# A hybrid encoder trunk on one core: gate projections as one stacked pass, attention inputs fetched block by block

## The chip, the cores and the metric

The kernel runs on one core of a Trainium2 chip. The metric is the device time of one execution, in microseconds. The engines named below are TensorE (PE in the rows; PEld is its weight load), VectorE (DVE), ScalarE (ACT), GpSimd (POOL) and SyncE (SP), which only issues transfers. ScalarE issues transfers too, in the same queue as its computing.

## What is computed

Two groups of tokens (512 and 256, together 768 in six tiles of 128) go through two layers and a final RMSNorm, all in fp32. A layer:

```python
h = rmsnorm(x, norm_g)
proj = h @ w_in
qa, ka, va, gfl, gbl, za, qb, kb, vb, zb, ma, mb = split(proj)
gf = log_sigmoid(gfl @ w_gate_f + b_gate_f) / 16     # rank 16 -> 512, forward decay
gb = log_sigmoid(gbl @ w_gate_b + b_gate_b) / 16     # the same for the backward direction
# branch A: gated linear attention, 4 heads (key 128, value 256), both directions
ya = (rmsnorm(o_forward + o_backward) * silu(za)) @ w_branch_a
# branch B: grouped-query attention, 16 query and 4 key heads of 64, RMSNorm and rotary on q, k
yb = (attention(rope(rmsnorm(qb)), rope(rmsnorm(kb)), vb) * silu(zb)) @ w_branch_b
x = x + (sigmoid(ma) * ya + sigmoid(mb) * yb) @ w_out
```

The gate path matters here: `gfl` and `gbl` have 16 columns each (32 together), and a small product takes them to 128 decays per head and direction. The other path is the one that prepares branch B: `q` and `kv` are read back from DRAM, squared, and summed over each head of 64.

## The kernel before

**Products in two parts.** A large product takes each operand as a high part (rounded to fp32r) and a low part (the rest), and makes three fp32r passes: high x high, high x low, low x high (`three_passes`, L510 to L512). Weights come through a ring of four slots. SyncE loads `w_raw`, ScalarE writes `w_hi` (`split`, L794), GpSimd writes `w_lo` (L1151), TensorE uses them and signals `w_used`. Weights are three blocks ahead (`SKEW = 3`). Smaller products are plain fp32, which shows as two records for each matmul.

**The gate projection.** A layer begins with `gemm_features(1)`: 128 columns of `w_in`, of which 32 are gate columns, in banks 6 and 7. VectorE copies 32 rows of the result to `gl_t` (L1536). Then follow the projections for `q`, `k` (`gemm_features(4)`) and `v` of branch A.

**The gate product.** `gla_gates` multiplies `gl_t` (32 rows) by the small weights `wg_fix` of one head in plain fp32:

```python
for d, start, n in ((0, 0, HALF), (0, HALF, TOK - HALF), (1, 0, TOK - HALF), (1, TOK - HALF, HALF)):
    z = 2 * HALF + d * TOK + start
    last = mm(ps[:, z:z + n], wg_fix[:, d, :], gl_t[:, start:start + n], start=True, stop=True)   # L594
```

GpSimd cuts `wg_fix` and the bias `bg_fix` out for each head (`gla_fix`). The first head's product stands alone in the gate stage, where ScalarE turns it into decays (`gate_magnitudes` L852, exponential, logarithm, exponential), with splits of background weights in between. Those of heads 1 to 3 run in level 3 of the head before.

**A linear-attention head** has ten levels (`GLA_STEPS`, n = 0 to 9). In level n TensorE makes a score product (L621, L609 in the last), then background tiles: the projections of branch B, `GLA_DONE` says up to which tile (4 in level 0, 11 in levels 1 to 5, then 10 or 11, 6 in the last). VectorE collects the product (`collect`, L1358 to L1365) and scales queries and keys for the next level (`doubled`, L1344 to L1350); ScalarE merges the keys (`merge_k`, L882), on which the next level's product waits. After level 9 VectorE drains and signals `a_ready` (L1388), and `gla_values` (L636) makes the head's output. Splits of background weights are spread over the levels (`GLA_START`), and in level 5 ScalarE stores a finished group of the background (`store`, L799 three times, then a DMA to `proj` in DRAM) before `merge_k`.

**The last head** also prepares branch B. In level 2 ScalarE issues everything at once in `fetch_qk`: four loads of `q`, two of `kv` (L816, 768 KB each), and four small parameters (L820) for the rope tables. From level 4 on it squares one token tile per level (`squares_of`, three ACTIVATEs, L904) and VectorE sums it (`square_sums`, L1435). The rope tables are made in level 3. The last tile's sums stand ahead of the drain for `a_ready`.

ScalarE, VectorE and GpSimd each work through their instructions in the order in which they are written; nothing overtakes a waiting one.

## Time and profile before

| | |
|---|---|
| median of 3 runs | 2178.04 us (2176.38 to 2178.86) |
| the profiled execution | 2178.59 us, span 2176.80 |
| TensorE busy | 2058.8 us, 95% of the span |
| ScalarE, VectorE, GpSimd busy | 858.1, 835.1, 659.3 us |
| mean granted clock of TensorE | 0.974 of full |
| moved by DMA | 157.07 MB, mean 72 GB/s |

Busy shares are means over stages with different limits, so they are read by stretch. The granted clock is given as a share of 2.4 GHz. A matmul's duration in a timeline overlaps its successor's; the pace is read from the distance between starts, or from the chain that ended last.

### The profile page before, as it was taken

To read this page: it belongs to the slowest core of one execution; us is meant where nothing else is said; L and a number is where in the kernel's file an instruction comes from. 1 tells how busy PE (TensorE), PEld (TensorE's weight loads), DVE (VectorE), ACT (ScalarE), POOL (GpSimd) and SP (SyncE) were. 2 spreads that over 40 slices of the span, in tenths; PEclk is the share of its full clock that TensorE was granted. 3 is DMA by queue.
4 is the path that set the end of the run, shared out by engine and by line. 5 is a ranking of instruction groups with operands and counts; after the bars stand their busy time and mean duration, and the time that the engine had idled before them with its cause. 6 is when DMAs were issued, how large, how long until landed. Compare 5 with 4: busy or idle time off the path is not lost.

```text
span 2176.8 us, 39353 instructions
## 1 busy us (share of the span) xinstructions
PE 2058.8 (95%) x13792; PEld 1896.9 (87%) x13792; DVE 835.1 (38%) x1158; ACT 858.1 (39%) x1712; POOL 659.3 (30%) x697
## 2 busy tenths in 40 slices
PE   5999999899999999999879999998999999999996
PEld 4988999899999998877779889998999999988785
DVE  3012555469432332323131035455693333323323
ACT  4113454443445454423221145444334555544222
POOL 1322222138432231322223322221583321213221
PEclk8999999999999999999979999999999999999998
DMA  3221212422111113331122111124221111142312
GB/s 122 68 58 49 66 53 63 149 70 65 53 43 41 58 43 127 117 117 54 34 69 61 51 54 61 60 68 142 76 61 45 44 58 39 60 145 87 113 59 84
DMA packets 116300, 157.07 MB, mean 72 GB/s; under 512 B 12960, under 2 KB 88992, under 8 KB 116192
## 3 DMA queue, kind: packets, MB, share of 16 engines
q1 hardware_dynamic: 78480, 96.18, 15.5%
q10 hardware_dynamic: 37712, 59.52, 7.8%
q8 instruction: 60, 0.98, 0.2%
q14 instruction: 48, 0.39, 0.1%
HBM read 124.20 MB, written 31.46 MB: 72 GB/s over the span
## 4 chain that ended last, share of the span: by engine, by line
PE 78%; issue 8%; POOL 6%; DVE 4%; ACT 2%; ACTq 1%; DMA 1%; DVEq 1%; POOLq 0%; SPq 0%
PE ps L510 10%; PE ps L512 10%; PE ps L511 10%; PE ps L548 8%; PE ps L550 8%; PE ps L549 8%; PE ps L691 6%; PE ps L621 5%; PE ps L636 3%; POOL w_lo L1151 3%; PE ps L675 3%; POOL rot L1190 2%; PE ps L574 2%; PE ps L667 2%; PE ps L668 2%
## 5 line engine op out<-in xcount | busy, mean ns | idle before, releaser
L1151 POOL TENSOR_TENSOR w_lo<-w_raw,w_hi 128x256 fp32r<-128x256 f32 (+2 forms) x531 | 525.2, 997 | 1466.9 <-ACT w_hi L794 1452.9
L548 PE MATMUL ps<-w_hi,act_hi 128*128 128x256 f32 x2112 | 625.5, 296 | 9.8 <-POOL w_lo L1151 7.0
L549 PE MATMUL ps<-w_lo,act_hi 128*128 128x256 f32 x2112 | 600.0, 284 | 0.0
L550 PE MATMUL ps<-w_hi,act_lo 128*128 128x256 f32 x2112 | 599.9, 284 | 0.0
L794 ACT ACTIVATE w_hi<-w_raw 128x256 fp32r<-128x256 f32 (+2 forms) x528 | 251.2, 485 | 583.8 <-PE ps L512 363.6
L548 PEld LDWEIGHTS ps<-w_hi,act_hi 128*128 128x128 f32 x2112 | 407.3, 193 | 15.1 <-POOL w_lo L1151 7.6
L549 PEld LDWEIGHTS ps<-w_lo,act_hi 128*128 128x128 f32 x2112 | 407.6, 193 | 0.6
L550 PEld LDWEIGHTS ps<-w_hi,act_lo 128*128 128x128 f32 x2112 | 406.7, 193 | 0.0
L1489 DVE TENSOR_REDUCE st<-ps 128x1 f32<-128x512 f32 (+1 forms) x160 | 110.4, 690 | 249.2 <-PE ps L668 248.2
L961 ACT ACTIVATE pr_t<-ps 128x512 f32<-128x512 f32 x160 | 95.6, 597 | 217.5 <-PE ps L675 217.5
L691 PE MATMUL ps<-v_grp,pr_t 128*128 128x64 f32 x1280 | 161.8, 269 | 1.4 <-DVE q L1495 1.4
L510 PE MATMUL ps<-w_hi,o_hi 128*128 128x512 f32 x384 | 154.8, 403 | 6.2 <-DVE o_lo L1297 3.3
L691 PEld LDWEIGHTS ps<-v_grp,pr_t 128*128 128x128 f32 x1280 | 156.8, 192 | 2.8 <-issue 2.8
L512 PE MATMUL ps<-w_hi,o_lo 128*128 128x512 f32 x384 | 150.6, 392 | 0.0
L511 PE MATMUL ps<-w_lo,o_hi 128*128 128x512 f32 x384 | 150.3, 391 | 0.0
L882 ACT ACTIVATE scaled<-scaled 128x768 f32<-128x768 f32 x64 | 53.3, 833 | 206.3 <-DVE scaled L1344 180.1
L953 ACT ACTIVATE pr<-ps,st 128x512 f32<-128x512 f32 (+1 forms) x192 | 116.9, 612 | 31.2 <-DVE st L1489 31.2
L621 PE MATMUL ps<-scaled 128*128 128x128 f32 x768 | 108.2, 294 | 16.7 <-ACT scaled L882 16.7
L621 PEld LDWEIGHTS ps<-scaled 128*128 128x128 f32 x768 | 100.9, 200 | 21.9 <-ACT scaled L882 17.3
L1360 DVE COPY_PREDICATED amat<-mask,ps 128x768 f32<-128x768 uint8 x56 | 58.0, 1036 | 134.7 <-PE ps L621 99.1
L510 PE MATMUL ps<-act_hi,w_hi 128*128 128x384 f32 x288 | 99.1, 344 | 6.3 <-DVEq L442 3.5
L511 PE MATMUL ps<-act_lo,w_hi 128*128 128x384 f32 x288 | 98.3, 341 | 0.0
(151 smaller groups left out, 3230.6 us busy)
## 6 DMA issues: line engine op xcount, KB each, us to landing
w_raw<-in_w_in SPq DMA_DIRECT2D x352, 128.0 KB, 2.1
proj<-stg ACTq DMA_DIRECT2D x36, 768.0 KB, 3.3
w_raw<-in_w_in SPq DMA_DIRECT2D x64, 256.0 KB, 2.7
w_raw<-in_w_branch_a SPq DMA_DIRECT2D x32, 256.0 KB, 2.6
w_raw<-in_w_branch_b SPq DMA_DIRECT2D x32, 256.0 KB, 2.6
w_raw<-in_w_out SPq DMA_DIRECT2D x32, 256.0 KB, 2.5
q<-proj ACTq DMA_DIRECT2D x8, 768.0 KB, 8.1
zb<-proj ACTq DMA_DIRECT2D x8, 768.0 KB, 7.3
```

Of the source, the lines that this page charges most:

```text
L510: mm(out, s_hi, m_hi, start=first, stop=False)
L511: mm(out, s_hi, m_lo, start=False, stop=False)
L512: return mm(out, s_lo, m_hi, start=False, stop=last)
L548: mm(out, act_hi[:, k, tok], w_hi[:, k % RING, 0:BGW], start=(k == 0 and t % 2 == 0), stop=False, skip_group_check=True)
L549: mm(out, act_hi[:, k, tok], w_lo[:, k % RING, 0:BGW], start=False, stop=False, skip_group_check=True)
L550: last = mm(out, act_lo[:, k, tok], w_hi[:, k % RING, 0:BGW], start=False, stop=(k == KT - 1), skip_group_check=True)
L621: last = mm(ps[:, j * P:(j + 1) * P], lhs, rhs, start=True, stop=True)
L691: last = mm(ps[:, 3 * HALF + t * DH:3 * HALF + (t + 1) * DH], pr_t[:, n % 2, (i * 2 + j) * P:(i * 2 + j + 1) * P], v_grp[:, key, :], start ...
L794: A(w_hi[:, slot, 0:width], w_raw[:, slot, 0:width], ACT.Copy).then_inc(s.w_hi_done, 1)
L953: last = A(pr[:, n % 2, i * w:(i + 1) * w], ps[:, n % 2 * HALF + i * w:n % 2 * HALF + (i + 1) * w], ACT.Exp, bias=nmax(n, i), accum_out=de ...
L1151: G.tensor_tensor(w_lo[:, slot, 0:width], w_raw[:, slot, 0:width], w_hi[:, slot, 0:width].bitcast(F32), ALU.subtract).then_inc(s.w_lo_done, 1)
L1489: V.tensor_reduce(out, view_ps(n % 2 * HALF, (HALF // k, k), (1, HALF // k)), AX.X, ALU.max, negate=True).then_inc(s.neg_max, 1)
```

## The change

Three things.

1. The gate projection loads 32 columns instead of 128 and stacks them: the 128 stationary columns hold the high part three times and the low part once (`gate_split`). One pass with the high part of the input and one with its low part replace the three passes (`gemm_gates`). The result has 128 rows.
2. `gl_t` and `wg_fix` become 128 rows of fp32r: rows 32 to 63 of `gl_t` hold what rounding took away, rows 64 to 95 of `wg_fix` the low part of the weights. The gate product is then one fp32r pass. The weights are loaded four times over (eight parameters instead of two), VectorE and GpSimd each get a chained subtraction.
3. In the last head the parameters are loaded in level 0, and the six blocks of `q` and `kv` one per level from level 1 to 6; each level waits for the block of the level before, and squares it as one column block over all six tiles. VectorE sums one block per level in levels 3 to 7, the rope tables move to level 8, and nothing is left ahead of `a_ready`.

```diff
-    gl_t = sb("gl_t", [2 * RANK, TOK], R_O + 11 * ROW)
+    gl_t = sb("gl_t", [P, TOK], R_O + 11 * ROW, F32R)
...
-    wg_fix = sb("wg_fix", [2 * RANK, 2, GK], R_G + NT * BGW * 4)
-    wg = sb("wg", [2 * RANK, 2, GH * GK], R_G + NT * BGW * 4 + 2 * GK * 4)
+    wg_fix = sb("wg_fix", [P, 2, GK], R_G + NT * BGW * 4, F32R)
+    wg = sb("wg", [P, 2, GH * GK], R_G + NT * BGW * 4 + 2 * GK * 4)
...
-                load_group(w_in, layer, C_GATES, P)
+                load_group(w_in, layer, C_GATES, GR)
...
-            def gemm_features(blocks):
+            def gemm_gates():
 
                 for k in range(KT):
                     pe.wait_ge(s.w_lo_done, at("w_lo_done"))
-                    for b in range(8 - 2 * blocks, 8):
+                    for half in range(2):
+                        if k == 0:
+                            pe.wait_ge(s.drained, at.peek("drained", half - 1))
+                        tok = slice(half * FH, (half + 1) * FH)
+                        mm(bank(6 + half, FH), w_hi[:, k % RING, 0:P], act_hi[:, k, tok], start=(k == 0), stop=False)
+                        last = mm(bank(6 + half, FH), w_hi[:, k % RING, 0:P], act_lo[:, k, tok], start=False, stop=(k == KT - 1))
+                        if k == KT - 1:
+                            last.then_inc(s.gemm_ready, 1)
+                    (last if k < KT - 1 else pe.drain()).then_inc(s.w_used, 1)
+                at.skip("drained", 2)
+
+            def gemm_features():
+
+                for k in range(KT):
...
-                gemm_features(1)
+                gemm_gates()
                 with at.repeat(2, "gla qk"):
-                    gemm_features(4)
+                    gemm_features()
...
+            def gate_split(k):
+
+                slot = (k + SKEW) % RING
+                act.wait_ge(s.w_slot[slot], at(f"w_slot{slot}", 16))
+                act.wait_ge(s.w_used, at("w_used"))
+                A(view(w_hi, slot * HALF, (GR, 3), (1, GR)), view(w_raw, slot * HALF, (0, 3), (1, GR)), ACT.Copy).then_inc(s.w_hi_done, 1)
...
-            def fetch_qk():
-
-                act.wait_ge(s.totals, at.peek("totals", 1))
-                all_stored()
-                for c in range(4):
-                    fetch(q, J_Q + c, c * BGW, D, 1, s.qkv_in)
-                for c in range(2):
-                    fetch(kv, J_K + c, c * BGW, HALF, 1, s.qkv_in)
-                param(cs_raw[:, 0, :, :], rope_cos)
-                param(cs_raw[:, 1, :, :], rope_sin)
-                param(g_qk[:, 0, :], rows_of(q_norm_g, layer * DH, DH))
-                param(g_qk[:, 1, :], rows_of(k_norm_g, layer * DH, DH))
-
-            def squares_of(t):
-
-                if t == 0:
-                    act.wait_ge(s.qkv_in, at("qkv_in", 6 * 16))
-                for part in range(3):
-                    src = view(q, t * D + part * HALF, (1, HALF)) if part < 2 else view(kv, t * HALF, (1, KVH * DH))
+            def fetch_qk(n):
+
+                if n == 0:
+                    param(cs_raw[:, 0, :, :], rope_cos)
+                    param(cs_raw[:, 1, :, :], rope_sin)
+                    param(g_qk[:, 0, :], rows_of(q_norm_g, layer * DH, DH))
+                    param(g_qk[:, 1, :], rows_of(k_norm_g, layer * DH, DH))
+                if n == 1:
+                    act.wait_ge(s.totals, at.peek("totals", 1))
+                    all_stored()
+                if n >= 2:
+                    act.wait_ge(s.qkv_in, at("qkv_in", 16))
+                if 1 <= n < 5:
+                    fetch(q, J_Q + n - 1, (n - 1) * BGW, D, 1, s.qkv_in)
+                if 5 <= n < 7:
+                    fetch(kv, J_K + n - 5, (n - 5) * BGW, HALF, 1, s.qkv_in)
+                if 2 <= n < 7:
+                    c = n - 2
+                    src = view(q, c * BGW, (D, NT), (1, BGW)) if c < 4 else view(kv, 0, (HALF, NT), (1, BGW))
                     act.wait_ge(s.sq_used, at("sq_used"))
-                    A(bank(2 + part, HALF if part < 2 else KVH * DH), src, ACT.Square).then_inc(s.sq_ready, 1)
+                    A(view_ps(2 * HALF, (BGW, NT), (1, BGW)), src, ACT.Square).then_inc(s.sq_ready, 1)
...
-                    if not more and n == 2:
-                        fetch_qk()
...
-                    if not more and 4 <= n:
-                        squares_of(n - 4)
+                    if not more and n < 8:
+                        fetch_qk(n)
...
-                param(wg[0:RANK, 0, :], bass.AP(w_gate_f.tensor, layer * (RANK * GH * GK), [[GH * GK, RANK], [1, GH * GK]]))
-                param(wg[RANK:2 * RANK, 1, :], bass.AP(w_gate_b.tensor, layer * (RANK * GH * GK), [[GH * GK, RANK], [1, GH * GK]]))
+                    if k + SKEW < KT:
+                        gate_split(k)
+                    else:
+                        split(k)
...
+            def gate_split(k):
+
+                slot = (k + SKEW) % RING
+                pool.wait_ge(s.w_hi_done, at("w_hi_done"))
+                G.tensor_tensor(w_hi[:, slot, 3 * GR:4 * GR], w_raw[:, slot, 0:GR], w_hi[:, slot, 0:GR].bitcast(F32),
+                                ALU.subtract).then_inc(s.w_lo_done, 1)
...
-                G.tensor_copy(wg_fix[:], view_32(wg, h * GK, (GH * GK, 2), (1, GK)))
                 G.tensor_copy(bg_fix[:], view(bg, h, (GH, 2)))
+                G.tensor_copy(wg_fix[:], view(wg, h * GK, (GH * GK, 2), (1, GK))).then_inc(s.pool_chain, 1)
+                pool.wait_ge(s.pool_chain, at("pool_chain"))
+                pool.sem_inc(s.passed, 1)
+                rows = slice(2 * GR, 3 * GR)
+                G.tensor_tensor(wg_fix[rows], view_rows(wg, 2 * GR, GR, h * GK, (GH * GK, 2), (1, GK)),
+                                wg_fix[rows].bitcast(F32), ALU.subtract)
                 pool.drain().then_inc(s.gla_fix, 1)
...
-                    if not more and n == 3:
+                    if not more and 3 <= n < 8:
+                        square_sums(n - 3)
+                    if not more and n == 8:
                         dve.wait_ge(s.param, at("param", 4 * 16))
                         dve.sem_inc(s.passed, 1)
                         rope_tables()
-                    if not more and 5 <= n:
-                        square_sums(n - 5)
-                if not more:
-                    square_sums(NT - 1)
                 at.skip("q_ready", 1)
...
-            def square_sums(t):
-
-                for part in range(3):
-                    heads = 8 if part < 2 else KVH
-                    stat = t * AH + part * 8 if part < 2 else NT * AH + t * KVH
-                    dve.wait_ge(s.sq_ready, at("sq_ready"))
-                    V.tensor_reduce(view(st_qk, stat, (1, heads)), view_ps((2 + part) * HALF, (DH, heads), (1, DH)),
-                                    AX.X, ALU.add).then_inc(s.sq_used, 1)
+            def square_sums(c):
+
+                dve.wait_ge(s.sq_ready, at("sq_ready"))
+                out = view(st_qk, c * GROUP, (AH, NT), (1, GROUP)) if c < KVH else view(st_qk, NT * AH, (KVH, NT), (1, KVH))
+                V.tensor_reduce(out, view_ps(2 * HALF, (BGW, NT), (DH, GROUP), (1, DH)), AX.X, ALU.add).then_inc(s.sq_used, 1)
...
-                    V.tensor_copy(gl_t[:, half * FH:(half + 1) * FH], ps[0:2 * RANK, (6 + half) * HALF:(6 + half) * HALF + FH]).then_inc(s.drained, 1)
+                    tok = slice(half * FH, (half + 1) * FH)
+                    V.tensor_copy(gl_t[:, tok], bank(6 + half, FH)).then_inc(s.dve_chain, 1)
+                    dve.wait_ge(s.dve_chain, at("dve_chain"))
+                    V.tensor_tensor(gl_t[GR:2 * GR, tok], ps[GR:2 * GR, (6 + half) * HALF:(6 + half) * HALF + FH],
+                                    gl_t[GR:2 * GR, tok].bitcast(F32), ALU.subtract).then_inc(s.drained, 1)
...
+                for copy in range(4):
+                    for d, w_gate in enumerate((w_gate_f, w_gate_b)):
+                        row = copy * GR + d * RANK
+                        param(wg[row:row + RANK, d, :], bass.AP(w_gate.tensor, layer * (RANK * GH * GK), [[GH * GK, RANK], [1, GH * GK]]))
```

## Rows read from the trace of the kernel before

**Rows 1.** Windows: busy time of each engine, granted clock, DMA share, GB/s.
```profile
270.00:330.00 60.00, 59.97 (x449) 57.13 (x449) 31.49 (x38) 29.61 (x52) 14.52 (x18) 1.00 0.19 58
390.00:450.00 60.00, 51.09 (x395) 50.00 (x394) 32.79 (x51) 22.90 (x52) 10.53 (x15) 0.94 0.45 141
```

**Rows 2.** Waits of TensorE over the whole span: us in total, times, longest.
```profile
PE ps L621 <- ACT scaled L882: 16.7, 3, 8.3
...
PE ps L636 <- DVEq L1388: 4.7, 2, 2.4
```

**Rows 3.** Timeline, ScalarE's queue in the last head, level 2.
```profile
403.03 3.25 ACTq L816 DMA_DIRECT2D q<-proj  x4
406.31 5.44 ACTq L816 DMA_DIRECT2D kv<-proj  x2
...
415.85 0.84 ACT L882 ACTIVATE scaled<-scaled 128x768 f32<-128x768 f32 x1 [13.05 <-issue]
```

**Rows 4.** Timeline, TensorE: head 1 to the start of head 2, then the last head.
```profile
272.41 1.50 PE L621 MATMUL ps<-qk_t,scaled 128*128 x12
...
286.52 1.50 PE L621 MATMUL ps<-scaled 128*128 128x128 f32 x12
...
291.90 2.84 PE L594 MATMUL ps<-gl_t,wg_fix 32*128 32x512 f32 x8
294.67 1.60 PE L621 MATMUL ps<-scaled 128*128 128x128 f32 x12
...
333.32 1.50 PE L621 MATMUL ps<-qk_t,scaled 128*128 x12
...
394.24 1.50 PE L621 MATMUL ps<-qk_t,scaled 128*128 128x128 f32 x12
...
467.88 0.38 PE L548 MATMUL ps<-w_hi,act_hi 128*128 128x256 f32 x1 [0.37 <-issue]
```

**Rows 5.** Chain that ended last, products of 384 columns: start, us.
```profile
48.30 0.17 PE ps L510
```

**Rows 6.** The same chain, products of 512 columns.
```profile
116.83 0.23 PE ps L511
```

**Rows 7.** Timeline of the gate stage, ScalarE and TensorE.
```profile
187.06 1.69 ACT L852 ACTIVATE gate<-ps,bg_fix 128x768 f32<-128x768 f32 x2 [7.41 <-PE ps L594]
...
202.33 0.58 PE L548 MATMUL ps<-w_hi,act_hi 128*128 128x256 f32 x1 [2.90 <-POOL w_lo L1151]
```

**Rows 8.** DMA issues: KB each, median us from issue to landing.
```profile
q<-proj ACTq DMA_DIRECT2D x8, 768.0 KB, 8.1
...
ma<-proj ACTq DMA_DIRECT2D x8, 768.0 KB, 4.7
...
kv<-proj ACTq DMA_DIRECT2D x4, 768.0 KB, 11.2
...
w_raw<-in_w_in SPq DMA_DIRECT2D x19, 64.0 KB, 1.9
```

**Rows 9.** Windows behind the gate product in head 0 of layer 2.
```profile
1308.00:1310.00 2.00, 2.00 (x11) 2.00 (x11) 0.16 (x1) 0.00 (x0) 0.00 (x0) 0.50 0.00 0
1310.00:1312.00 2.00, 2.00 (x16) 2.00 (x16) 2.00 (x3) 0.28 (x1) 0.00 (x0) 0.82 0.00 0
```

**Rows 10.** Timeline, ScalarE and VectorE in levels of head 1 and the last head.
```profile
298.33 0.85 ACT L882 ACTIVATE scaled<-scaled 128x768 f32<-128x768 f32 x1 [6.26 <-DVE scaled L1344]
...
422.73 0.34 DVE L1420 TENSOR_TENSOR cs<-cs_raw,g_qk 128x192 f32<-128x192 f32 x1
...
426.38 1.04 DVE L1360 COPY_PREDICATED amat<-mask,ps 128x768 f32<-128x768 uint8 x1 [0.34 <-DVEq L1426]
...
430.68 1.55 ACT L799 ACTIVATE stg<-ps 128x512 f32<-128x512 f32 x3
...
433.75 1.61 DVE L1435 TENSOR_REDUCE st_qk<-ps 128x8 f32<-128x512 f32 x3
...
434.46 1.20 ACT L904 ACTIVATE ps<-q 128x512 f32<-128x512 f32 x2
```

More of the change, by code:

```diff
@@ L53 @@
 RANK = 16
+GR = 2 * RANK
 GATE_NORM = 16.0
@@ L353, in view, with view_rows @@
         return bass.AP(t, start, [[row, P]] + [list(d) for d in dims])
+    def view_rows(t, first, n, start, *dims):
+        row = 1
+        for size in t.shape[1:]:
+            row *= size
+        return bass.AP(t, first * row + start, [[row, n]] + [list(d) for d in dims])
     def rows_of(a, start, n):
@@ L495, in _ @@
                         load_group(w, layer, g * HALF)
-            load_group(w_in, 0, C_GATES, P, blocks=SKEW)
+            load_group(w_in, 0, C_GATES, GR, blocks=SKEW)
             for t in range(NT):
@@ L552, in background @@
                         last.then_inc(s.w_used, 1)
-            def gemm_features(blocks):
+            def gemm_gates():
                 for k in range(KT):
                     pe.wait_ge(s.w_lo_done, at("w_lo_done"))
-                    for b in range(8 - 2 * blocks, 8):
+                    for half in range(2):
[10 more added lines that the diff above has]
+                for k in range(KT):
+                    pe.wait_ge(s.w_lo_done, at("w_lo_done"))
+                    for b in range(8):
                         if k == 0:
                             pe.wait_ge(s.drained, at.peek("drained", b + 1 - 8))
-                        col = slice((b // 2 + blocks - 4) * P, (b // 2 + blocks - 3) * P)
+                        col = slice(b // 2 * P, (b // 2 + 1) * P)
                         tok = slice(b % 2 * FH, (b % 2 + 1) * FH)
@@ L567, in gemm_features @@
                     (last if k < KT - 1 else pe.drain()).then_inc(s.w_used, 1)
-                at.skip("drained", 2 * blocks)
+                at.skip("drained", 8)
             def turn_step(src, m):
@@ L1126, in _ @@
                 for k in range(KT):
-                    split(k, HALF if k + SKEW < KT else P)
+                    if k + SKEW < KT:
+                        split(k)
+                    else:
+                        gate_split(k)
                     if k == 1:
@@ L1226, in _ @@
             for k in range(SKEW):
-                split(k - SKEW, P)
+                gate_split(k - SKEW)
             with at.repeat(DEPTH, "layer"):
@@ L1232, in _ @@
                 for k in range(KT):
-                    split(k, P if k + SKEW < KT else HALF)
+                    if k + SKEW < KT:
+                        gate_split(k)
+                    else:
+                        split(k)
                 with at.repeat(4, "gla projections"):
                     splits()
-                pool.wait_ge(s.param, at("param", (2 + 2 * GH) * 16))
+                pool.wait_ge(s.param, at("param", (8 + 2 * GH) * 16))
                 pool.sem_inc(s.passed, 1)
@@ L1259, in _ @@
                 for k in range(KT):
-                    split(k, HALF if k + SKEW < KT else P)
+                    if k + SKEW < KT:
+                        split(k)
+                    else:
+                        gate_split(k)
                 phase_ends()
```

30 lines of the change are left out of this document (12 added, 18 removed).

## The prediction

> **What bounds the kernel now.** I read the busy shares by stretch first. In an ordinary linear-attention head TensorE is busy 59.97 of 60 us; in the stretch of the last head of the layer it is busy only 51.09 of 60, while the DMA share goes from 0.19 to 0.45 [rows 1]. So in ordinary heads, time goes only if TensorE work goes; in the last head something else sets the end.
>
> The waits say what. TensorE stands at L621 (the score product of a level) for the ScalarE copy L882 (`merge_k`), 8.3 us at the longest, once in each of the two layers, and at L636 (`gla_values`) for VectorE's queue, 2.4 us, once in each [rows 2]. The timeline of ScalarE's queue shows the cause of the first. From 403.03 on it issues four loads of `q` (3.25 us) and two of `kv` (5.44 us), then the four parameters of the rope tables until 415.85, where the next L882 runs [rows 3]. L882 stood behind 12.8 us of issuing, in a queue full of its own transfers, while VectorE had long scaled its input. The second wait is the block of `square_sums` that VectorE still has ahead of the drain that feeds `a_ready`.
>
> How much is that in all? I compare whole heads by the starts of TensorE work [rows 4]. Head 1 runs from 272.41 to the next head's first product at 333.32, 60.91 us, of which the gate product L594 takes 294.67 - 291.90 = 2.77 us; the last head has none. So an undisturbed last head should take 58.14 us. It takes 467.88 - 394.24 = 73.64 us, of which 0.37 is the drain behind it. Excess: 73.64 - 0.37 - 58.14 = 15.1 us. The two waits give 10.7 of it; the rest is the lower clock after each of them and a small stall at the store. The second layer repeats both waits with the same lengths [rows 2].
>
> **Part 1, the gate projection.** Before: 8 blocks x 2 halves x 3 passes = 48 matmuls of 384 columns. After: two passes, 32. At full clock one takes 0.17 us of the chain [rows 5]; the stretch at half clock with which the group starts I take to be equally long with either count, so the 16 that go are priced at full clock: 16 x 0.17 = 2.7 us, **5.4 us** in two layers. (If they went at half clock it would be twice that, which the range holds.) Is something late instead? The three-deep ring of split weights: the copy and the subtraction get narrower, and the first wide block is ordered several blocks ahead; I find it ready about when the gates end, inside the half microsecond that TensorE spends on its drain and loop between the groups. The loads become 32 columns (128 B a row) instead of 128. One of 64 KB lands after 1.9 us now [rows 8], and the last narrow one has over 4 us before its split is due; at twice 1.9 us it would still be in time. If the first wide block is late by all of one copy and subtraction, 1 us a layer is lost: the bounds of this part are 3.4 and 5.4, and I take the upper.
>
> VectorE's two drains become four short instructions; they free banks 6 and 7, which the next group needs only after 18 matmuls (18 x 0.17 = 3.1 us). Without that cover the two added ones would cost about 1 us. ScalarE issues eight weight parameters instead of two. Even in the full queue of rows 3 four parameters took 4.1 us (411.75 to 415.85), so six more cost at most 6.2 us; what is queued behind them is the split of the next group's fourth block, which TensorE wants after three blocks of 24 matmuls, 72 x 0.17 = 12 us. GpSimd's `gla_fix` gains a chained wait and a subtraction, an estimated 1 to 2 us; it runs in level 1 and L594 comes at the end of level 3, two levels later. All of these at nothing.
>
> **Part 2, the gate product L594.** It is now a plain fp32 product over 32 rows, 1,536 columns, 2.77 us [rows 4]. After, it is one fp32r product over 128 rows with the same columns. An fp32r product of 512 columns takes 0.23 us of the chain [rows 6], so 1,536 take 0.69 us. Saved: 2.08 us each. Six lie in heads where TensorE is full: **12.5 us**. Two lie in the gate stage, where the chain begins with them: ScalarE's L852 waits for L594 at 187.06, and TensorE later waits 2.90 us for a split that stands behind that chain, until 202.33 [rows 7]. The chain starts 2.08 us earlier and keeps its length: **4.2 us**. The bounds are 0 (if the new form ran at the old rate) and 2.77 us each (if it vanished); I take 2.08 because every other fp32r product of the trace runs at this pace.
>
> **Part 3, the clock.** Outside stretches with idle time, the granted clock falls three times in the trace, each time at or right behind an L594 (near 187, 1307 and 1431 us; one of the three stands in the rows). With TensorE busy 2.00 of 2.00 it shows 0.50, the lower of its two levels (1.2 of 2.4 GHz), then 0.82 on the way back [rows 9]: (0.50 + 0.18) x 2 = 1.4 us lost. Two of these lie in full heads. The new product fills all rows and is four times shorter, so I expect no fall: **2.8 us**, between 0 and 3.2.
> The Trainium skill, "TensorE: Matmul & The Clock Gate", section "Seeing it yourself", shows the clock falling after matmuls have stopped, and its section "What's actually happening" ties it to how busy TensorE has been. Read as idle time alone, this term would be 0 and the time 2129; the rows, which fall without idle time, disagree with that reading.
>
> **Part 4, the last head.** Six transfers of 768 KB are now issued one at a time, one per level from level 1 on; ScalarE waits for the last one before it issues the next; the four parameters come in level 0. Does each transfer fit into a level? A level takes 291.90 - 286.52 = 5.4 us of TensorE, 1.5 of it the score product [rows 4]. Six at once land after 8.1 us (`q`) and 11.2 us (`kv`); `ma`, fetched with spacing and in the same form, after 4.7 us [rows 8]. ScalarE comes back to the wait one level later, about 5.0 us after the issue. So it nearly never waits. Its queue then holds, per level, L882 0.85, up to two splits (an estimated 0.8), an issue (0.5) and one square of 1,536 columns: two of 512 take 1.20 us now [rows 10], so three times 512 in one, about 1.5 us. L882 is wanted 298.33 - 294.67 = 3.7 us after its level's score product begins [rows 4, 10]; ScalarE, held until then by the second split and the square, is free at about 2.1 to 2.5 us. One place doesn't fit: level 5 begins with the store (three copies, 1.55 us [rows 10]), which stands behind the square of level 4, which stands behind VectorE's sum of the block before. VectorE's sum ends about 1.65 + 3.0 + 1.6 = 6.2 us into level 4, the square 1.5 us later, 2.3 us after the next level's score product has started; the first bank is copied at about 2.9, and TensorE wants it at 1.5. New stall: 1.4 us, against 0.5 now (estimates, all of them).
>
> VectorE: five sums of 1,536 columns at about 1.6 us (three reduces of a tile take 1.61 us [rows 10]) instead of six; with an estimated 3.3 us of level work that is 4.9 us, under 5.4. The rope tables take 3.65 us with their drain, from 422.73 to the copy at 426.38 [rows 10]; they move to level 8, where VectorE has about as much time free before it must take up the last product; an estimated 0.4 us late at most, and `a_ready` then comes just as TensorE arrives, since the reduces ahead of it are gone. So of 15.1 us, 1.4 stay: 13.7 x 2 = **27.4 us**. Bounds: nothing saved (the transfers land as late as now) to 30.2.
>
> **Sum.** 5.4 + 12.5 + 4.2 + 2.8 + 27.4 = 52.3 us. The profiled execution took 2178.59 (span 2176.80 and 1.79 around it): 2126.3. It was 0.55 above the median of 2178.04: 2125.7. I say 2126.
>
> **The rivals.**
> *The fetches set the pace of the last head.* ScalarE's loop is then: a transfer lands, the next is issued, square, copy, wait. A level can't be shorter than one landing. With 8.1 us, the present median of `q`, six levels are 2.8 us longer, less about 3 of slack: 14 us a layer, which takes back the 27.4: about 2153. For it: ScalarE waits in order and weights are loaded beside it. Against: the long landings are those of six in flight at once. In a mild form (5.9 us) it costs 1 to 2 us a layer and is in my range. 0.12.
> *The same, and slower than before.* At a landing of 11.2 us, `kv`'s median, six levels are 5.9 us longer each, 32 us a layer after slack: 64 - 52.3 = 12 us slower, 2190. It decides from about 10.2 us of landing on. That number exists only with six in flight. 0.02.
> *The heads don't give the time back.* If VectorE and ScalarE really pace the levels, the 12.5 and 2.8 us go: 2141. Against: 59.97 of 60, and no L621 waits in those heads [rows 1, 2]. 0.08.
> *The clock stays as it is.* Falls go on after the gate product (2.8 us), and the new stall in level 5 brings one of about 2 us in each layer: 2133. 0.18.
> *As forecast.* 0.60, by itself 2121 to 2131.
>
> The range takes in the clock rival and the mild fetch rival and stops short of the strong one: 2118 to 2144. What a measurement of this kernel can tell from no change is 0.2%, 4.4 us; of the cases only the fetch rival at a landing near 10.2 us comes there, and I leave it 0.01. Faster 0.97, same 0.01, slower 0.02.
>
> **What would show it.** L594 as four records of about 0.7 us together per head; heads of about 58.8 us from first product to first product, equal in both layers; no wait at L621 for L882 over 1 us; ScalarE's issues of `q` and `kv` at 0.4 to 0.6 us each, landing under 5.5; no wait at L636; a stall of about 1.4 us at the first background matmul after the level-5 product; granted clock 1.00 throughout the last head. Wrong would make it: landings of 7 us or more, a level-5 stall that lowers the clock, or a gate stage whose chain starts no earlier because the wider `gla_fix` ends it.

## The result, and the profile after

The changed kernel takes 2124.3 us (median of 4 runs, 2122.36 to 2125.05) against 2178.45 us for the kernel before on the same chip: a ratio of 0.9752, with a 95% interval of 0.9735 to 0.9769. That is 54 us saved where 52 were forecast. The profiled execution took 2124.74 us, its span is 2122.9 us against 2176.8, and its mean granted clock 0.983 against 0.974.

I cut both traces at the same instructions (first gate matmul, first q/k/v matmul, gate product, first score product of each head, first matmul behind the last head) and subtracted. Two numbers in a cell are the two layers; three are heads 0, 1 and 2.

| stretch | before, us | after, us | saved in all | forecast |
|---|---|---|---|---|
| gate projection | 11.35, 11.98 | 9.20, 7.93 | 6.2 | 5.4 |
| q, k, v projections | 136.65, 136.56 | 136.68, 136.65 | -0.1 | 0 |
| gate stage (gate product to first score product) | 27.33, 26.17 | 24.38, 24.16 | 5.0 | 4.2 |
| heads 0 to 2 of layer 1 | 60.93, 60.91, 60.92 | 58.73, 58.65, 58.64 | 6.7 | 12.5 + 2.8 = 15.3 for both layers |
| heads 0 to 2 of layer 2 | 62.22, 60.92, 62.23 | 58.72, 58.67, 58.66 | 9.3 | (in the row above) |
| last head with the drain behind it | 73.64, 73.55 | 59.92, 59.92 | 27.35 | 27.4 |
| all the rest | | | -0.5 | 0 |

The busy time in windows of 60 us (engine busy time with the number of instructions, then the granted clock, the DMA share and GB/s) is read as in [rows 1], for the changed kernel, first around an ordinary head and then in the last one:

```profile
270.00:330.00 60.00, 59.97 (x461) 58.44 (x461) 32.74 (x40) 29.63 (x52) 16.63 (x21) 1.00 0.20 61
380.00:440.00 60.00, 58.52 (x449) 57.01 (x448) 39.55 (x53) 28.07 (x51) 11.97 (x16) 1.00 0.47 149
```

TensorE was busy 51.09 us in such a stretch of the last head and is busy 58.52 now; the 1.48 us that is missing is one stall, in the next fence. The ordinary head was full and is full: it got shorter by the 2.06 us of work that left it, and by 0.2 us beside that work.

TensorE's timeline (start, busy time, line, operation, tiles, count, and in brackets the idle time ahead of it with its releaser), answers to [rows 4]: the gate product is one group of four, and from its start to that of its successor it takes 284.47 - 283.76 = 0.71 us where it was 2.77. The last head begins at 381.64 and the first matmul behind it is at 441.56.

```profile
283.76 0.87 PE L616 MATMUL ps<-gl_t,wg_fix 128*128 128x512 f32 x4
284.47 1.50 PE L643 MATMUL ps<-scaled 128*128 128x128 f32 x12
...
381.64 1.50 PE L643 MATMUL ps<-qk_t,scaled 128*128 128x128 f32 x12
...
406.35 1.50 PE L643 MATMUL ps<-scaled 128*128 128x128 f32 x12
...
409.33 0.38 PE L555 MATMUL ps<-w_hi,act_hi 128*128 128x256 f32 x1 [1.48 <-ACT stg L828]
...
441.56 0.38 PE L555 MATMUL ps<-w_hi,act_hi 128*128 128x256 f32 x1 [0.34 <-issue]
```

No score product (L643) waits for `merge_k` (L911) any more, and no `gla_values` matmul (L658) for VectorE's queue; [rows 2] had 16.7 and 4.7 us there. Of TensorE's waits in these stages these entries of the list of waits remain (us in total, times, longest): the splits of the gate stage, and the stores, of which the two of 1.48 us, one in each last head, are the longest.

```profile
PE ps L555 <- POOL w_lo L1184: 8.6, 4, 3.6
...
PE ps L555 <- ACT stg L828: 4.5, 4, 1.5
```

ScalarE's queue in levels 1 to 5 of the last head answers to [rows 3]. An issue takes 0.38 to 0.41 us instead of 8.7 us for six in a row, `merge_k` waits for its data and not for issuing, and one square of 1,536 columns takes 1.46 us:

```profile
390.45 0.41 ACTq L845 DMA_DIRECT2D q<-proj  x1
394.02 0.85 ACT L911 ACTIVATE scaled<-scaled 128x768 f32<-128x768 f32 x1 [3.63 <-DVE scaled L1392]
...
395.33 0.40 ACTq L845 DMA_DIRECT2D q<-proj  x1
395.77 1.46 ACT L933 ACTIVATE ps<-q 128x1536 f32<-128x1536 f32 x1
...
405.88 0.38 ACTq L845 DMA_DIRECT2D q<-proj  x1
407.31 1.45 ACT L933 ACTIVATE ps<-q 128x1536 f32<-128x1536 f32 x1 [1.55 <-DVE st_qk L1479]
408.70 1.55 ACT L828 ACTIVATE stg<-ps 128x512 f32<-128x512 f32 x3
```

The square that starts at 407.31 had waited 1.55 us for VectorE's sum; the store's copies (L828) stand behind it, and TensorE stands behind the first of them. The DMA issues (size of one, median time from issue to landing) answer to [rows 8]: 8.1 and 11.2 us became 4.8 and 4.9.

```profile
q<-proj ACTq DMA_DIRECT2D x8, 768.0 KB, 4.8
...
kv<-proj ACTq DMA_DIRECT2D x4, 768.0 KB, 4.9
...
w_raw<-in_w_in SPq DMA_DIRECT2D x19, 16.0 KB, 1.8
```

### The profile page after: what moved, and what is told of

Its sections match the earlier page's. It is cut to its first block, busy times and chain, and to the rows that moved or that the text cites. A ratio compares the mean times of both kernels' runs of the same rounds, so it can differ in the third digit from the quotient of the medians.

```text
span 2122.9 us, 39205 instructions
## 1 busy us (share of the span) xinstructions
PE 2023.0 (95%) x13728; PEld 1872.6 (88%) x13728; DVE 836.0 (39%) x1136; ACT 854.8 (40%) x1686; POOL 662.2 (31%) x705
## 3 DMA queue, kind: packets, MB, share of 16 engines
q10 hardware_dynamic: 38096, 59.92, 8.2%
## 4 chain that ended last, share of the span: by engine, by line
PE 81%; issue 6%; POOL 6%; DVE 3%; ACT 2%; DMA 1%; DVEq 0%; ACTq 0%; SPq 0%; POOLq 0%
PE ps L517 10%; PE ps L519 10%; PE ps L518 10%; PE ps L555 8%; PE ps L557 8%; PE ps L556 8%; PE ps L713 6%; PE ps L643 5%; PE ps L658 3%; PE ps L697 3%; POOL w_lo L1184 3%; POOL rot L1232 2%; PE ps L596 2%; PE ps L689 2%; PE ps L690 2%
## 5 line engine op out<-in xcount | busy, mean ns | idle before, releaser
L1184 POOL TENSOR_TENSOR w_lo<-w_raw,w_hi 128x256 fp32r<-128x256 f32 (+1 forms) x512 | 515.7, 1016 | 1324.0 <-ACT w_hi L816 1322.1
L816 ACT ACTIVATE w_hi<-w_raw 128x256 fp32r<-128x256 f32 (+1 forms) x512 | 246.1, 490 | 545.5 <-PE ps L519 321.8
L911 ACT ACTIVATE scaled<-scaled 128x768 f32<-128x768 f32 x64 | 53.3, 833 | 162.4 <-DVE scaled L1392 161.3
L643 PE MATMUL ps<-scaled 128*128 128x128 f32 x768 | 102.4, 283 | 0.0
L643 PEld LDWEIGHTS ps<-scaled 128*128 128x128 f32 x768 | 96.8, 192 | 0.3
L697 PE MATMUL ps<-ident,pr 128*128 128x128 f32 x640 | 95.9, 272 | 0.0
L517 PEld LDWEIGHTS ps<-w_hi,o_hi 128*128 128x128 f32 x384 | 72.9, 190 | 24.2 <-issue 5.8
```

The lines of the kernel that those rows point to most:

```text
L517: mm(out, s_hi, m_hi, start=first, stop=False)
L643: last = mm(ps[:, j * P:(j + 1) * P], lhs, rhs, start=True, stop=True)
L697: last = nc.tensor.transpose(ps[:, 2 * HALF + j * P:2 * HALF + (j + 1) * P], pr[:, n % 2, j * P:(j + 1) * P], ident[:])
L816: A(w_hi[:, slot, 0:width], w_raw[:, slot, 0:width], ACT.Copy).then_inc(s.w_hi_done, 1)
L1184: G.tensor_tensor(w_lo[:, slot, 0:width], w_raw[:, slot, 0:width], w_hi[:, slot, 0:width].bitcast(F32), ALU.subtract).then_inc(s.w_lo_done, 1)
```

## The experiments

Beside these runs the kernel before took 2176.0 to 2177.1 us, beside the changed kernel 2178.45. Where a run is compared with the changed kernel's 2124.3 below, the difference in time is therefore good to about 2 us; the stretches of the traces are finer. The diffs are cut to the lines that carry the change, and `...` marks a cut.

**One half of the change each.** The first kernel has the new gate path and the old fetch; the second the old gate path and the new fetch. The diff is the first one's edit on ScalarE; on VectorE `square_sums` and `rope_tables` go back to their old levels. The second is the kernel before with the reverse of it.

```diff
+                    if not more and n == 2:
+                        fetch_qk()
...
-                    if not more and n < 8:
-                        fetch_qk(n)
+                    if not more and 4 <= n:
+                        squares_of(n - 4)
```

> The stacked gate projection and the fp32r gate product, with the fetches and squares of the last head as they were. If the parts simply add, by the step lengths of the two traces: gate projection 6, gate stage 5, heads 16, so 27 us faster than before (about 2151), and the last head keeps its wait of 8.3 us at the level-3 product and its 2.4 us ahead of the values. Rival (the parts cover one another: a shorter chain gives the last head more or less to wait for): the last head's 73.6 us change by more than 1 us.

> The fetches and squares block by block, with the gate projection in three passes and the gate product in plain fp32 over 32 rows. If the parts add: 27 us faster than before (about 2151), last head 59.9 us. The plain gate product is there again eight times: my theory of the clock says that one to four of them are followed by a granted clock of 0.50 while TensorE is busy. The rival (the falls came by chance or from the idle times elsewhere) says none in a second profile.

The gate path alone: 2149.71 us against 2177.08, ratio 0.9874 (0.9851 to 0.9897), 27.4 us less. The fetch alone: 2150.27, ratio 0.9875 (0.9859 to 0.9892), 26.8 us less. Together 54.2 us, what the whole change gives: as times the halves add up. In the first kernel both waits of [rows 2] are still there, from its list of waits:

```profile
PE ps L643 <- ACT scaled L911: 15.8, 3, 7.9
...
PE ps L658 <- DVEq L1438: 4.7, 2, 2.4
```

Its last heads take 73.08 and 71.57 us, 0.56 and 1.98 less than before, so 2.5 us of the last head's gain are to be had by the gate path too: the wait is 0.4 us shorter, and in layer 2 the clock does not fall a second time behind the wait for `a_ready`. In the second kernel the other heads take 60.93 to 60.94 us, and one 62.24, as before, and its last heads 59.95 and 59.92: the fetch alone gives the whole of that term. As stretches the halves add less neatly than as times. The 2.5 us are in both; against them, the stretch from the last head of layer 1 to the gate projection of layer 2, whose code is the same everywhere, takes 644.9 and 645.6 us in the two kernels against 642.1 before and 644.4 after.

**The gate product: type or rows?** The 128 stacked rows stay, the operands are plain fp32. (The subtractions then give zeros in the rows for the low parts; the product's value is that of plain fp32.)

```diff
-    gl_t = sb("gl_t", [P, TOK], R_O + 11 * ROW, F32R)
+    gl_t = sb("gl_t", [P, TOK], R_O + 11 * ROW)
...
-    wg_fix = sb("wg_fix", [P, 2, GK], R_G + NT * BGW * 4, F32R)
+    wg_fix = sb("wg_fix", [P, 2, GK], R_G + NT * BGW * 4)
```

> The changed kernel with the gate product in plain fp32 over 128 rows (64 of them hold zeros, since nothing is rounded away; the result is the same sum). It separates length from rows. Price of the plain product: 8 x 2.06 = 16.5 us slower than the changed kernel (about 2141). On the clock: if the 32 used rows made it fall, it stays at 1.00 behind all eight products; if the 2.8 us of plain fp32 made it fall, it falls behind some of them and heads with a fall are about 1.4 us longer.

2137.38 us, ratio 0.982 (0.9803 to 0.9836): 13.1 us slower than the changed kernel, where 16.5 were expected. Between the starts of its neighbours the product now takes 2.58 us, from TensorE's timeline:

```profile
285.70 2.74 PE L616 MATMUL ps<-gl_t,wg_fix 128*128 128x512 f32 x8
288.28 1.50 PE L643 MATMUL ps<-scaled 128*128 128x128 f32 x12
```

Its heads take 60.53 us, 1.88 more than 58.65, and the gate stages 26.27 and 26.25, 1.9 and 2.1 more: 15.2 us; its gate projections are 1.4 us shorter, because their first matmuls run at half clock for less time. So of the 2.06 us per product the type gives 1.87, and 0.19 comes from filling the rows: the plain product over 32 rows is slower than the plain product over 128. No run shows why.

**Three passes again in the gate projection.**

```diff
                         mm(bank(6 + half, FH), w_hi[:, k % RING, 0:P], act_hi[:, k, tok], start=(k == 0), stop=False)
+                        mm(bank(6 + half, FH), w_hi[:, k % RING, 0:P], act_lo[:, k, tok], start=False, stop=False)
                         last = mm(bank(6 + half, FH), w_hi[:, k % RING, 0:P], act_lo[:, k, tok], start=False, stop=(k == KT - 1))
```

(It adds the low part of the input once too often.)

> The changed kernel with a third pass in the stacked gate projection (the product with the low part of the input is added twice, so the output is not the reference's). It prices the 16 matmuls alone. At full clock: 2.7 us a layer, 5.4 in all, gate projection 2.7 us longer in both layers. Rival: the lengths of the two layers (9.2 and 7.9 us now) move by different amounts, because the time at half clock at the start of the group varies by more than the matmuls cost.

2129.38 us, ratio 0.9782 (0.9765 to 0.9798), 5.1 us slower. The projections take 10.78 and 10.90 us against 9.20 and 7.93: 1.6 and 3.0 us more, unequal, as the rival said, and 4.6 in all. Of the eighteen projections of nine kernels with the short form, fourteen take 7.7 to 8.6 us, three 9.1 to 9.2 and one 6.6; their mean is 8.1, that of the six of three kernels with three passes 11.05. The difference is how much of one runs at half clock, as the windows of the changed kernel at the start of the group show (the granted clock is the third number from the end), layer 1 and then layer 2:

```profile
36.00:38.00 2.00, 2.00 (x8) 2.00 (x7) 0.00 (x0) 0.28 (x1) 0.25 (x1) 0.50 0.06 12
38.00:40.00 2.00, 2.00 (x7) 2.00 (x7) 0.00 (x0) 0.57 (x2) 0.29 (x2) 0.50 0.45 126
40.00:42.00 2.00, 2.00 (x9) 2.00 (x9) 0.00 (x0) 0.34 (x2) 0.46 (x2) 0.62 0.76 166
...
1086.00:1088.00 2.00, 2.00 (x6) 2.00 (x7) 0.00 (x0) 0.48 (x2) 0.25 (x1) 0.50 0.06 11
1088.00:1090.00 2.00, 2.00 (x9) 2.00 (x9) 0.00 (x0) 0.35 (x2) 0.51 (x2) 0.65 0.24 34
```

The share of the last row gives the moment of the return: layer 1 stays at half clock until about 41.5, 6.2 us into the group (0.62 is 1.5 us at 0.50 and 0.5 at 1.00), layer 2 until about 1089.4, 3.4 us into it.

**Six transfers at once, but in the new places.** All six are issued in level 1. Squares and sums follow one level later than in the changed kernel, and the rope tables stand in level 3 instead of 8 (VectorE's part of the edit is not shown).

```diff
-                if n >= 2:
-                    act.wait_ge(s.qkv_in, at("qkv_in", 16))
-                if 1 <= n < 5:
-                    fetch(q, J_Q + n - 1, (n - 1) * BGW, D, 1, s.qkv_in)
-                if 5 <= n < 7:
-                    fetch(kv, J_K + n - 5, (n - 5) * BGW, HALF, 1, s.qkv_in)
-                if 2 <= n < 7:
-                    c = n - 2
+                    for c in range(4):
+                        fetch(q, J_Q + c, c * BGW, D, 1, s.qkv_in)
+                    for c in range(2):
+                        fetch(kv, J_K + c, c * BGW, HALF, 1, s.qkv_in)
+                if n == 3:
+                    act.wait_ge(s.qkv_in, at("qkv_in", 6 * 16))
+                if 3 <= n < 8:
+                    c = n - 3
```

> The changed kernel with all six fetches issued together in level 1, one wait for all of them in level 3, squares in levels 3 to 7, rope tables in level 3. Nothing waits for a landing before level 3. If the issuing itself stalls ScalarE (its queue is full of its own transfers, 8.7 us for six in the trace of before), the level-2 key copy comes 4 to 6 us late, TensorE waits 3 to 5 us for it in each layer, and the kernel is 6 to 10 us slower than the changed one. If the old stall came from waiting for the landings, this form costs nothing: same as the changed kernel.

2138.56 us, ratio 0.9829 (0.9814 to 0.9844), 14 us slower than the changed kernel. ScalarE's queue shows the block of issuing back, and `merge_k` behind it (8.97 us in which ScalarE's computing waited for nothing that the profile shows but its own issues):

```profile
389.41 3.35 ACTq L845 DMA_DIRECT2D q<-proj  x4
392.79 5.42 ACTq L845 DMA_DIRECT2D kv<-proj  x2
398.32 0.84 ACT L911 ACTIVATE scaled<-scaled 128x768 f32<-128x768 f32 x1 [8.97 <-issue]
```

```profile
399.22 2.07 PE L643 MATMUL ps<-scaled 128*128 128x128 f32 x8 [4.33 <-ACT scaled L911]
...
415.52 0.39 PE L555 MATMUL ps<-w_hi,act_hi 128*128 128x256 f32 x1 [2.17 <-ACT stg L828]
```

The second fence is TensorE's timeline of the same kernel: 4.33 us of waiting, and 2.17 us at the store. The last heads take 68.61 and 66.86 us, 8.7 and 6.9 more. The direction is that of the theory, and the wait of 4.33 us is in its range of 3 to 5. The size, 6 to 10 us, was forecast too small: the lower clock behind the wait and the price of the tables' new place were not in it. The next kernel has squares, sums and tables in the same levels as this one and differs only in how they are issued and waited for; it is 10.7 us faster, timed in the same comparison, and that is about the price of six at once against pairs.

**Two at a time.** Pairs are issued in levels 1, 3 and 5; squares, sums and tables stand where they did in the run above.

```diff
+                if n in (3, 5, 7):
+                    act.wait_ge(s.qkv_in, at("qkv_in", 2 * 16))
+                if n in (1, 3):
+                    for c in (n - 1, n):
+                        fetch(q, J_Q + c, c * BGW, D, 1, s.qkv_in)
+                if n == 5:
+                    for c in range(2):
+                        fetch(kv, J_K + c, c * BGW, HALF, 1, s.qkv_in)
```

> The changed kernel with the fetches issued in pairs in levels 1, 3 and 5, waited for two levels later, squares in levels 3 to 7, rope tables in level 3. If only a full queue makes issuing slow, a pair costs 0.8 to 1 us, there is no wait for the key copy, and the time is that of the changed kernel within 2 us. If each issue beside another transfer stalls (2 us or more), 1 to 3 us slower per layer.

2127.84 us, ratio 0.9775 (0.976 to 0.979), 3.5 us slower. From its ScalarE timeline, a pair is issued in 1.00 us, and it lands after 5.8 us (`q`) and 6.4 us (`kv`):

```profile
390.41 1.00 ACTq L845 DMA_DIRECT2D q<-proj  x2
```

No wait of TensorE stands behind a pair. Yet the last heads take 62.75 and 61.19 us, 2.8 and 1.3 more: the level-5 product waits 0.40 us for `merge_k`, and the store stall is 2.17 us instead of 1.48. Neither comes from the fetches. VectorE makes the rope tables in level 3 here, and what follows in its queue is late: the next collecting copy starts at 403.99, where it is 402.69 in the changed kernel. ScalarE's `merge_k` waits for VectorE behind that, and so does the square ahead of the store; in layer 1 the clock then falls behind the stall besides. VectorE's row first, then ScalarE's:

```profile
403.99 1.03 DVE L1410 COPY_PREDICATED amat<-mask,ps 128x768 f32<-128x768 uint8 x1 [0.35 <-DVEq L1474]
405.89 0.84 ACT L911 ACTIVATE scaled<-scaled 128x768 f32<-128x768 f32 x1 [2.46 <-DVE scaled L1394]
```

**The splits of the gate stage.** This goes beyond the change. In the changed kernel TensorE stands 0.77 and 3.54 us in each gate stage for the subtraction that follows a split:

```profile
191.59 0.38 PE L555 MATMUL ps<-w_hi,act_hi 128*128 128x256 f32 x1 [0.77 <-POOL w_lo L1184]
...
197.54 0.39 PE L555 MATMUL ps<-w_hi,act_hi 128*128 128x256 f32 x1 [3.54 <-POOL w_lo L1184]
```

```diff
                 split(0, BGW)
                 gate_exps()
-                gate_logs()
                 split(1, BGW)
+                gate_logs()
+                split(2, BGW)
                 copy_k(0)
+                split(3, BGW)
                 gate_decays()
-                for i in range(2, GLA_FIRST // NT):
+                for i in range(4, GLA_FIRST // NT):
```

> The changed kernel with the gate stage of ScalarE in another order: split 1 ahead of the logarithm, split 2 behind it, split 3 ahead of the last exponential. In the changed kernel TensorE waits 0.77 and 3.54 us there for splits queued behind table loads, and runs about 3 us at half clock behind it. I expect both waits gone and the decay chain 0.5 to 1 us later: 4 to 6 us a layer, 8 to 12 us in all (about 2114). Rival: the decay chain sets the end of the stage, the wait moves to the level-1 product, and nothing is gained.

2114.75 us, ratio 0.9715 (0.9701 to 0.9728), 9.6 us below the changed kernel. The gate stages take 19.18 and 19.17 us, 5.1 less on average; a wait of 0.87 us is left in each. The waits give 3.4 us of it; the rest is the clock, which stays at 1.00 in both stages now and was at 0.50 for 3.4 us behind the longer wait in the changed kernel. The splits had stood in ScalarE's order behind the logarithms and the decays, for which they have no need.

**No square in level 4.** On top of that order, level 4 has no square, so that nothing stands ahead of the store in level 5; the tables move to level 5.

```diff
-                if 2 <= n < 7:
-                    c = n - 2
+                if n in (2, 3, 5, 6, 7):
+                    c = n - 2 if n < 4 else n - 3
...
-                    if not more and 3 <= n < 8:
-                        square_sums(n - 3)
-                    if not more and n == 8:
+                    if not more and n in (3, 4, 6, 7, 8):
+                        square_sums(n - 3 if n < 5 else n - 4)
+                    if not more and n == 5:
```

> As the run with splits earlier, and no square in level 4 of the last head: squares in levels 2, 3, 5, 6, 7, sums in 3, 4, 6, 7, 8, rope tables in level 5. The stall of 1.48 us at the store goes (3 us in both layers). VectorE is about 1.5 us over its level in level 5; with slack behind it I expect at most 0.5 us of wait. 2 to 3 us faster than with splits earlier, too little for the times to tell, but the waits in the profile show it. Rival: the tables in level 5 bring a wait for the key copy as long as the stall that goes.

2112.7 us, ratio 0.9705 (0.9692 to 0.9719). The last heads take 58.97 and 58.96 us, 0.95 less. The store stall of 1.48 us is gone and a smaller one took its place, at the level-6 product. It is the wait that the rival named, at over a third of the size: `merge_k` waits for VectorE, which stood at the rope tables in level 5. VectorE, ScalarE and TensorE in turn:

```profile
409.55 1.03 DVE L1410 COPY_PREDICATED amat<-mask,ps 128x768 f32<-128x768 uint8 x1 [0.35 <-DVEq L1474]
411.45 0.84 ACT L911 ACTIVATE scaled<-scaled 128x768 f32<-128x768 f32 x1 [3.63 <-DVE scaled L1394]
412.43 1.58 PE L643 MATMUL ps<-scaled 128*128 128x128 f32 x12 [0.56 <-ACT scaled L911]
```

This is the fastest of all: 64 us below the kernel before, 11.6 below the changed one and 2 below the run with the splits earlier (a distance that single runs of the two overlap; the stretches carry it).

**The clock: length or rows?** The product after is both shorter and wider, so its clock proves nothing on which of the two did it. Both kernels here are that with plain fp32 and do the four matmuls three times over, which gives the same values; the second uses only rows 0 to 31, which leaves the low part of the weights out. The second pair of lines is the second kernel's alone:

```diff
-                for d, start, n in ((0, 0, HALF), (0, HALF, TOK - HALF), (1, 0, TOK - HALF), (1, TOK - HALF, HALF)):
+                for _ in range(3):
+                    for d, start, n in ((0, 0, HALF), (0, HALF, TOK - HALF), (1, 0, TOK - HALF), (1, TOK - HALF, HALF)):
...
-                        last = mm(ps[:, z:z + n], wg_fix[:, d, :], gl_t[:, start:start + n], start=True, stop=True)
+                        last = mm(ps[:, z:z + n], wg_fix[0:GR, d, :], gl_t[0:GR, start:start + n], start=True, stop=True)
```

> The run with plain fp32 over 128 rows, with the gate product made three times in each place (same operands, same output). So far the clock fell behind 6 of 16 plain products over 32 rows and behind 0 of 8 over 128 rows, each 2.8 us long. If the used rows decide, the clock stays at 1.00 behind all eight, though TensorE now does plain fp32 for 8.3 us at a time. If the length of plain fp32 decides, it falls behind most of the eight.

> The same, with only the first 32 rows of both operands in the product (the part of the gate input that came through the low half of the weights is left out). Everything else is as in its partner. If the used rows decide, the clock falls behind all eight or all but one, with TensorE busy throughout, and each head is over 1.5 us longer than its partner's. If it is chance, both runs look alike.

128 rows: 2182.11 us, ratio 1.0026 (1.0015 to 1.0038). 32 rows: 2222.35 us (2 runs), ratio 1.0217 (1.0169 to 1.0264), 40 us more. Windows of 2 us of one head, first the kernel with 128 rows (the next product starts at 238.55), then that with 32 (all four within the product):

```profile
236.00:238.00 2.00, 2.00 (x8) 1.30 (x7) 0.00 (x0) 0.00 (x0) 0.00 (x0) 1.00 0.00 0
238.00:240.00 2.00, 2.00 (x15) 1.64 (x14) 0.00 (x0) 0.00 (x0) 0.00 (x0) 1.00 0.00 0
```

```profile
238.00:240.00 2.00, 2.00 (x8) 1.29 (x7) 0.00 (x0) 0.00 (x0) 0.04 (x1) 1.00 0.48 131
240.00:242.00 2.00, 2.00 (x5) 1.11 (x4) 0.00 (x0) 0.00 (x0) 0.00 (x0) 0.55 0.00 0
242.00:244.00 2.00, 2.00 (x5) 1.19 (x4) 0.00 (x0) 0.00 (x0) 0.00 (x0) 0.50 0.00 0
244.00:246.00 2.00, 2.00 (x3) 0.66 (x2) 0.00 (x0) 0.00 (x0) 0.00 (x0) 0.50 0.00 0
```

TensorE is busy 2.00 of 2.00 us in every row. With 128 rows the clock stays at 1.00 through about 8 us of this product, in all eight places; with 32 rows it falls to 0.50 in all eight, for 10 to 17 us, and a head takes 71 to 72 us against 65.7. With the product done once over 32 rows it fell in 3 of 8 places in each of two kernels (before, and the new fetch alone); once over 128 rows, in fp32r or plain, in none of the 8 places of any of eight kernels. So it is the narrow operand with which the clock falls. The length alone does not lower it, but over 32 rows the longer product made the fall certain: 8 of 8 places instead of 3 of 8.

## Why the prediction was right

It said 2126, and 2124.3 was measured, in the likeliest case's own range of 2121 to 2131. The mechanisms held. That the total is within 2 us is in part luck: stretches that depend on when the clock comes back gave 1.6 us more than their terms (gate projection and gate stage), and cost 2.3 elsewhere. The steps one by one:

- **Gate projection, 5.4.** Measured 6.2, and 4.6 when the third pass was put back; the means over all kernels, 11.05 and 8.1, give 5.9. Sixteen matmuls at full clock were about the right price. The assumption that the stretch at half clock at its start is equally long with either count was the loose end: it is 6.2 us in one layer and 3.4 in the other of the same kernel, and can move this term by about as much as it is off, 0.8. The cover of everything priced at nothing (the wide first split, eight parameters, four drains) held: the q, k, v groups take 136.7 us as before, and the narrow loads land after 1.8 us.
- **Gate product, 12.5 and 4.2.** 2.06 us each against 2.08 forecast. Where this time goes was right too: heads of 58.65 us where 58.8 was forecast, full before and after. Another 0.2 us of a head, 1.1 in all, went outside the product, and did so with the plain product over 128 rows as well (60.53 - 2.58 = 57.95 against 60.91 - 2.77 = 58.14), so it goes with the rows and not with the type. The reason given (fp32r at the pace of the other fp32r products) is nine tenths of it; the rest, 0.19 us, comes from the rows, which the fp32 variant showed and the prediction did not have. The gate stage gave 2.95 and 2.01 us. Its chain, from the start of the gate product to the matmul that had waited for the last split, is 1.88 and 1.87 us shorter (18.18 before in both layers, 16.30 and 16.31 after), against 2.08 forecast. The rest, 1.1 us in layer 1, is the clock behind that wait: TensorE ran at 0.50 there for 5.9 us before and for 3.4 after, which the sum did not have. The 6 us behind the wait, the kernel before first, then the changed one (granted clock third from the end):

```profile
202.33:208.33 6.00, 6.00 (x28) 6.00 (x29) 0.00 (x0) 0.42 (x1) 2.74 (x4) 0.51 0.34 90
```

```profile
197.54:203.54 6.00, 6.00 (x37) 6.00 (x38) 0.00 (x0) 0.42 (x1) 2.76 (x4) 0.72 0.36 91
```

  The fall near 187 costs nothing here: layer 2 has none behind its product and the same 18.18 us, since TensorE waits for the split in any case.
- **The clock, 2.8.** The two full heads with a fall were 1.31 us longer than their neighbours, and that is gone: 2.6. "Fills all rows and is four times shorter" named two causes together; the last pair of runs settles that it takes the narrow operand. The Trainium skill, "TensorE: Matmul & The Clock Gate", section "What's actually happening", lets the clock follow how busy TensorE has been. Read as busy time, no fall would come in either kernel of that pair; the one with 128 rows agrees, the one with 32 rows, busy 2.00 of 2.00 us at 0.50, does not. The rival in which the clock stays as it is had 0.18 and is refuted: no fall behind any of the eight products over 128 rows, and the new stall of 1.48 us did not lower it either: 1.00 over the whole last head.
- **The last head, 27.4.** 27.35. Landing under 5.5 us: 4.8 and 4.9. Issues at 0.4 to 0.6: 0.38 to 0.41. The stall at the store, 1.4 estimated: 1.48, in both layers, by the chain that was named (sum, square, first copy). Sizes that were off within it: the sum takes 1.75 us, not 1.6, the square 1.46, not 1.5. The last heads of the kernel with the new fetch alone are as short, so the term is the fetch's.
- **The fetch rivals** (0.12 and 0.02) rested on the landings of six transfers in flight. Six in flight land at 8.0 and 11.9 us, two at 5.8 and 6.4, one at 4.8 and 4.9. The long landing belongs to the number in flight, as argued.
- **What the sum left out.** In layer 1 the branch after attention takes longer. Windows there, the changed kernel first, then the kernel before at about the same work:

```profile
836.00:840.00 4.00, 2.17 (x9) 1.65 (x10) 2.27 (x4) 2.03 (x4) 0.55 (x1) 0.50 1.10 364
840.00:844.00 4.00, 4.00 (x12) 3.09 (x13) 0.00 (x0) 0.00 (x0) 0.71 (x1) 0.55 1.10 348
```

```profile
862.00:866.00 4.00, 1.82 (x9) 1.46 (x10) 2.41 (x4) 2.16 (x4) 0.68 (x1) 0.80 1.09 366
866.00:870.00 4.00, 4.00 (x20) 3.28 (x20) 0.69 (x1) 0.60 (x1) 0.59 (x1) 1.00 1.10 348
```

The work is the same and has similar short idle stretches, but the clock comes back about 6 us later, at 843.6 against 863.6 with the work 26.3 us apart: 12 matmul records in 4 us where there were 20. That stretch with the rest of the layer costs 2.3 us; the start and the second layer's tail gave 1.7 back. It is no price of the change: with the same code there, the stretch from the last head of layer 1 to the next gate projection takes 641.9 to 645.6 us in the ten other kernels, 642.0 in the one with the plain product over 128 rows. What decides when the clock comes back there was not tried, and stays open. It is the same looseness as in the gate projection and the gate stage, and with it single terms are good to about a microsecond.

## What to carry to other kernels

When an engine both computes and issues transfers, count how many of its transfers are in flight: six of 768 KB in a row kept its queue issuing for 8.7 us here, with TensorE waiting behind it, while one per level cost 0.4 us each and landed in half the time. Look as well at what moves with them: the rope tables, moved to level 3 or 5, brought waits of TensorE that the transfers themselves did not. A matmul over a quarter of the rows cost more than its own time here, 1.3 us of a head each time the clock fell behind it; stack the high and low parts into the idle rows. And before measuring a saving on the full engine, measure the order of the one beside it: moving three splits ahead of the logarithms, the copy and the decays in ScalarE's order gave 9.6 us, more than the whole gate projection.

## What was not expected of the hardware

- At the gate product the granted clock fell with TensorE busy all the time, and only with operands of 32 rows: 3 of 8 places in each of two kernels with 2.8 us of such work, 8 of 8 with three times that work, none with 128 rows.
- A plain fp32 product over 32 rows takes longer than over 128 rows: 2.77 against 2.58 us for the same 1,536 columns.
- Issuing does not cost in proportion to the number: 0.4 us for one transfer of 768 KB, 1.00 for two, but 3.35 for four and 5.42 for the two that followed.
